# Entry of the feed-forward part of a hybrid layer: order of the first sums, the norm and the last output-projection block

## The chip, the cores and the metric

The kernel runs on one core of one Trainium2 chip. The metric is the device time of one execution in microseconds (us); a kernel's time is the median of several executions.

## The reference

The kernel computes one inference step of one encoder layer, in float32, for 1024 prompt frames and 32 sample frames (1056 token columns in all). Eight heads of latent attention and eight heads of a recurrent mixer (RWKV-7) read the same normalised projection; their outputs are concatenated into `mix` (1024 wide). What matters here is the tail:

```python
mix = concat([rmsnorm(attn, attn_out_g), rw])
h = x + mix @ w_out                       # 1024 x 1024
u = rmsnorm(h, norm_ffn_g)
return h + (silu(u @ w_gate) * (u @ w_up)) @ w_down    # D_FF = 2816
```

## The kernel before, in words

The program has three stages, each with its own hand-written instruction stream per engine and semaphores between them: `layer_inputs` (projection, latents, recurrent mixer and sample attention), `prompt_attention`, and `tail`. All of the change lies in `tail` (L2081 to L2549). Data is held transposed: 128 features on the partitions and the 1056 tokens on the free axis, so a 1024-wide tensor is eight blocks of 128 x 1056.

**Output projection.** It is made in eight blocks `u` (L2215 to L2226), each of three column groups `n` of 352 tokens, each a chain of eight matmuls over `k` (blocks 0 and 1 have their upper four done in the attention stage already, so only four). Block `u` uses PSUM banks 3b to 3b+2 with b = u % 2, and the weight buffer `wo[b]`: there are two, `g.wo`, filled with blocks 0 and 1 by the stage before. SP loads block u into `wo[u % 2]` when block u-2 is done (L2159 to L2161), behind the loads of x (`hT`, in three parts), of `g_ffn` and of the first two units of feed-forward weights (L2147 to L2158). VectorE adds each bank to x in `hT` (L2425, semaphore `h_ok`), and after each block squares it (L2427) and adds the square to `acc` (L2428).

**The norm.** Its gain is applied at once and its row factor late. `uT` = `hT` times `g_ffn`, eight blocks, four by ScalarE (L2341) and four by VectorE (L2431), is written over `mixT`, so it has to wait until TensorE has read `mixT`. The row factor takes its own way: TensorE sums `acc` over the partitions (`row_sums`, L2227), VectorE scales and adds epsilon (L2440, L2441), GpSimd (POOL) raises to the power -0.5 (L2373), ScalarE spreads the nine columns into diagonal matrices (L2351), TensorE multiplies ones by them (`row_factors`, L2233), and VectorE copies the result to `rb` (L2448). Everything that leaves the first feed-forward products is then multiplied by `rb` on VectorE.

**The feed-forward products** are made by a Strassen-Winograd scheme: the 2 x 2 blocks of weights (A11, A12, A21, A22) and tokens (B11u, B12u, B21u, B22u; the first index is the upper or lower half of the features, the second the half of the columns, cut at HT = 528) give seven products with three sums of weights, S1, S2, S4 (and S3 in the place of A21), made by POOL for each unit (L2379 to L2384), and three sums of tokens, T1u, T2u, T4u (and T3 in the place of B12u), made once by VectorE (L2433 to L2437). A unit is a pair of 128-wide output blocks of the gate or of the up weights; `it` = 2u + nh counts units and column halves (NW = 264). For each `it` TensorE makes, in this order, X = A11 B11 (`p1_ps`), Y = S2 T2 (`p6_ps`), Z = S3 B12 (`p7_ps`), W = S1 T1 (`p5_ps`), then X += A12 B21, Z += A22 T4, W += S4 B22. `product` (L2239) records every one of these matmuls under L2241; each product is four matmuls of 264 columns, which the trace shows as eight.

In the first `it` TensorE waits for all of `h_ok` and for the four lower blocks of uT (`u_lo`) before X, makes `row_sums` behind X, and makes `row_factors` ahead of the second `it`. POOL's program begins with the power (it waits for `ms_ok`), and its sums for unit 0 come behind it:

```python
        pool.wait_ge(s["ms_ok"], 2)                                                        # L2372
        tt(row_ms[:, :], row_ms[:, :], minus_half, ALU.pow).then_inc(s["r_ok"], 1)
        for u in range(UNITS):
            ...
            pool.wait_ge(s[f"w_in{b}"], 32 * (u // 2 + 1))
            tt(S1, A21, A22, ALU.add).then_inc(s["s1_ok"], 1)
```

The order on every engine is written out by hand, so each engine does its instructions strictly in the order of its program.

Of the kernel before, what the change touches and what calls it, by code (L numbers as in the profile page):

```python
# [7 lines left out]
ALU = mybir.AluOpType  # L8
ACT = mybir.ActivationFunctionType
# [2071 lines left out]
def tail(nc, g, io, phase):  # L2081
# [20 lines left out]
    g11 = sb("g11", [P, NW])  # L2102
    diag = hid_[:, 9 * TOK:9 * TOK + TT_ * P].rearrange("p (t n) -> p t n", t=TT_)
    ones = hid_[:, 6 * TOK:6 * TOK + P]
    wo = [w[:, :, :] for w in g.wo]

    u_sum = [sb(f"u_sum{i}", [P, KH * HT]) for i in range(3)]
    wA = [sb(f"wA{i}", [P, 2 * KD * P + 3 * KH * P]) for i in range(2)]
# [18 lines left out]
    S1d = u_sum[1][:, 3 * NW:3 * NW + 10 * P].rearrange("p (k n) -> p k n", k=10), u_sum[2][:, FH * P:12 * P].rearrange("p (k n) -> p k n", k=1)  # L2127
    Alo, Ahi = (w[:, 0:FB * P].rearrange("p (k n) -> p k n", k=FB) for w in wA)

    names = """x_in0 x_in1 x_in2 g_in in0 in1 waited zero ps_done h_ok sq_ok acc_ok ssq_ps ms_ok r_ok diag_ok rb_ps rb_ok u_lo u_hi h_st  # L2130
        t1_ok t2_ok t3_ok t4_ok w_in0 w_in1 s1_ok s2_ok s3_ok s4_ok p1_ps p6_ps p7_ps p5_ps x_ps z_ps w_ps
        p1_ok y_done u3_ok c22_ok x_done z_done w_done th11 th22 th21 th12 c_ok hid_ok
        a11_in a12_in a21_in a22_in e1_ok e2_ok e3_ok e4_ok f1_ok f2_ok f3_ok f4_ok q1_ps q6_ps q7_ps q5_ps q4_ps q2_ps q3_ps
# [9 lines left out]
    def _(sp):  # L2143
        def load(u, b):
            sp.dma_start(wo[b], io.w_out[u]).then_inc(s[f"in{b}"], 16)

        for i, (a, b) in enumerate(X_PARTS):  # L2147
            sp.dma_start(hT[:, a:b], io.x_cols[a:b].rearrange("k p n -> p k n")).then_inc(s[f"x_in{i}"], 16)
        sp.dma_start(g_ffn[:, :], io.g_ffn).then_inc(s["g_in"], 16)

        def load_unit(u):
# [4 lines left out]

        load_unit(0)
        load_unit(1)  # L2158
        for u in range(2, KD):  # L2159
            sp.wait_ge(s["ps_done"], 3 * (u - 1))  # L2160
            load(u, u % 2)  # L2161
        sp.wait_ge(s["h_ok"], 3 * KD)
        sp.dma_start(io.y.rearrange("k p n -> p k n"), hT).then_inc(s["h_st"], 16)
        for u in range(2, UNITS):
# [49 lines left out]
    def _(pe):  # L2214
        for u in range(KD):  # L2215
            b = u % 2
            if u >= 2:
                pe.wait_ge(s[f"in{b}"], 16 * (u // 2))
            for n in range(3):
                if u >= 2:  # L2220
                    pe.wait_ge(s["h_ok"], 3 * (u - 2) + n + 1)
                depth = KD if u >= 2 else 4
                for k in range(depth):
                    last = pe.matmul(pb[3 * b + n][:, 0:TN], wo[b][:, k, :], g.mixT[:, k, n * TN:(n + 1) * TN],  # L2224
                                     start=k == 0 and u >= 2, stop=k == depth - 1, skip_group_check=u < 2)
                last.then_inc(s["ps_done"], 1)  # L2226
        def row_sums():  # L2227
            pe.wait_ge(s["acc_ok"], KD)
            for t, w in enumerate(width):
# [16 lines left out]
        for u in range(UNITS):  # L2246
            b = u % 2
            pe.wait_ge(s[f"w_in{b}"], 32 * (u // 2 + 1))
            for nh in range(2):
                it, c = 2 * u + nh, slice(nh * NW, nh * NW + NW)  # L2250
                X, Y, Z, W = (4 * (it % 2) + i for i in range(4))
                half = lambda t: (lambda k: t[:, k, c])
                left = lambda w: (lambda k: w[:, k, :])
                A11, A12, S3, A22 = (ab[b][:, a, KH * d:KH * d + KH] for a in range(2) for d in range(2))
                if it == 0:
                    pe.wait_ge(s["h_ok"], 3 * KD)
                    pe.wait_ge(s["u_lo"], KH)
                if it == 1:
                    row_factors()
                    pe.wait_ge(s["rb_ok"], 3)  # L2260
                if it >= 2:
                    pe.wait_ge(s["x_done"], it - 1)
                product(X, left(A11), half(B11u), KH, "p1_ps")
                if it == 0:
                    row_sums()
                pe.wait_ge(s["s2_ok"], u + 1)
                if it == 0:
                    pe.wait_ge(s["t2_ok"], 1)
                if it >= 2:
                    pe.wait_ge(s["y_done"], it - 1)  # L2270
                product(Y, left(sw[b][:, 1]), half(T2u), KH, "p6_ps")
                pe.wait_ge(s["s3_ok"], u + 1)
                if it == 0:
                    pe.wait_ge(s["t3_ok"], 1)
                if it >= 2:
                    pe.wait_ge(s["z_done"], it - 1)
                product(Z, left(S3), half(B12u), KH, "p7_ps")
                pe.wait_ge(s["s1_ok"], u + 1)
                if it >= 2:
                    pe.wait_ge(s["w_done"], it - 1)  # L2280
                product(W, left(sw[b][:, 0]), half(T1u), KH, "p5_ps")
                pe.wait_ge(s["p1_ok"], it + 1)
                product(X, left(A12), half(B21u), KH, "x_ps", first=False)
                if it == 0:
                    pe.wait_ge(s["t4_ok"], 1)
                pe.wait_ge(s["u3_ok"], it + 1)
                product(Z, left(A22), half(T4u), KH, "z_ps", first=False)
                pe.wait_ge(s["s4_ok"], u + 1)
                pe.wait_ge(s["c22_ok"], it + 1)
                product(W, left(sw[b][:, 2]), half(B22u), KH, "w_ps", first=False)  # L2290
# [43 lines left out]

    @block.scalar
    def _(act):
        act.wait_ge(s["ps_done"], 3 * KD)
        act.wait_ge(s["g_in"], 16)
        for k in (0, 1, 4, 5):
            act.wait_ge(s["h_ok"], 3 * k + 3)  # L2340
            act.activation(uT[:, k, :], hT[:, k, :], ACT.Copy, scale=g_ffn[:, k:k + 1]).then_inc(s["u_hi" if k >= KH else "u_lo"], 1)  # L2341
        for u in range(UNITS):
            for nh in range(2):
                it = 2 * u + nh
# [24 lines left out]
    @block.gpsimd  # L2369
    def _(pool):  # L2370
        tt = pool.tensor_tensor
        pool.wait_ge(s["ms_ok"], 2)  # L2372
        tt(row_ms[:, :], row_ms[:, :], minus_half, ALU.pow).then_inc(s["r_ok"], 1)  # L2373
        for u in range(UNITS):
            b = u % 2
            A11, A12, A21, A22 = (ab[b][:, a, KH * d:KH * d + KH] for a in range(2) for d in range(2))
            S1, S2, S4 = (sw[b][:, i] for i in range(3))
# [29 lines left out]
    def _(dve):  # L2407
# [7 lines left out]
        dve.memset(ones, 1.0).then_inc(s["zero"], 1)  # L2415
        dve.memset(row_ms[:, :], 1.0).then_inc(s["zero"], 1)
        dve.wait_ge(s["zero"], 3)
        for u in range(KD):
            for i, (a, _) in enumerate(X_PARTS):
                if u == a:  # L2420
                    dve.wait_ge(s[f"x_in{i}"], 16)
            for n in range(3):
                c = slice(n * TN, (n + 1) * TN)
                dve.wait_ge(s["ps_done"], u * 3 + n + 1)
                tt(hT[:, u, c], pb[3 * (u % 2) + n][:, 0:TN], hT[:, u, c], ALU.add).then_inc(s["h_ok"], 1)  # L2425
            dve.wait_ge(s["h_ok"], u * 3 + 3)
            named(tt(hsq, hT[:, u, :], hT[:, u, :], ALU.mult), "sq_ok", u + 1)  # L2427
            named(tt(acc, acc, hsq, ALU.add), "acc_ok", u + 1)  # L2428
        dve.wait_ge(s["g_in"], 16)
        for k in (2, 3, 6, 7):  # L2430
            dve.tensor_scalar(uT[:, k, :], hT[:, k, :], g_ffn[:, k:k + 1], None, ALU.mult).then_inc(s["u_hi" if k >= KH else "u_lo"], 1)  # L2431
        dve.wait_ge(s["u_lo"], KH)
        named(tt(T1u, B12u, B11u, ALU.subtract), "t1_ok", 1)  # L2433
        dve.wait_ge(s["u_hi"], KH)
        named(tt(T2u, B22u, T1u, ALU.subtract), "t2_ok", 1)
        tt(B12u, B22u, B12u, ALU.subtract).then_inc(s["t3_ok"], 1)
        tt(T4u, B21u, T2u, ALU.subtract).then_inc(s["t4_ok"], 1)  # L2437
        full = TOK // P
        dve.wait_ge(s["ssq_ps"], 1)
        dve.tensor_scalar(row_ms[:, 0:full], pb[6][:, 0:full], 1.0 / D, EPS, ALU.mult, ALU.add).then_inc(s["ms_ok"], 1)  # L2440
# [234 lines left out]
```

## Time and profile before

| | |
|---|---|
| median of 3 runs | 1986.47 us (1984.15 to 1988.41) |
| the profiled execution's own time | 1982.82 us |
| its span in the profile | 1981.0 us |
| TensorE busy with matmuls | 1841.3 us (93%) |
| VectorE, ScalarE, POOL busy | 1000.0, 361.7, 688.0 us |
| mean granted TensorE clock | 0.967 of full |

Engines: PE is TensorE's matmuls, PEld its weight loads, DVE is VectorE, ACT is ScalarE, POOL is GpSimd, SP is SyncE, whose rows are issues of DMAs. Times in rows are microseconds from the start of the span, and a bracket at the end of a row says how long the engine had been idle and whose instruction ended that. The granted clock PEclk is a share of 2.4 GHz, so 0.5 is 1.2 GHz. The `tail` stage begins at about 1006.7 us.

### The profile page before, as it was taken

To read this page: it belongs to the slowest core of one execution; us is meant where nothing else is said; L and a number is where in the kernel's file an instruction comes from. 1 tells how busy PE (TensorE), PEld (TensorE's weight loads), DVE (VectorE), ACT (ScalarE), POOL (GpSimd) and SP (SyncE) were. 2 spreads that over 40 slices of the span, in tenths; PEclk is the share of its full clock that TensorE was granted. 3 is DMA by queue.
4 is the path that set the end of the run, shared out by engine and by line. 5 is a ranking of instruction groups with operands and counts; after the bars stand their busy time and mean duration, and the time that the engine had idled before them with its cause. 6 is when DMAs were issued, how large, how long until landed. Compare 5 with 4: busy or idle time off the path is not lost. (4 is left out here: it accounts for less than half of the span.)

```text
span 1981.0 us, 33700 instructions
## 1 busy us (share of the span) xinstructions
PE 1841.3 (93%) x14303; PEld 1362.0 (69%) x14303; DVE 1000.0 (50%) x1742; ACT 361.7 (18%) x898; POOL 688.0 (35%) x495
## 2 busy tenths in 40 slices
PE   6799899999999796999989799999999999899998
PEld 3456566556566664555556488888888888688887
DVE  0657677677676785555533434343443443423522
ACT  1322332332323332333300100000000000000000
POOL 2543544544543453644500212222222221352622
PEclk9999999999999798999989899999999999899999
DMA  9545455554542101610031201111111111233331
GB/s 387 170 154 181 144 160 160 166 160 148 177 150 76 52 8 32 163 43 11 1 151 43 88 22 43 43 43 43 43 43 43 43 43 51 91 125 110 125 102 63
DMA packets 74071, 193.26 MB, mean 98 GB/s; under 512 B 19641, under 2 KB 48137, under 8 KB 66882
## 3 DMA queue, kind: packets, MB, share of 16 engines
q1 hardware_dynamic: 66578, 114.23, 18.2%
q10 hardware_dynamic: 7344, 76.88, 11.2%
q8 instruction: 114, 1.87, 0.4%
q14 instruction: 35, 0.29, 0.1%
HBM read 162.97 MB, written 20.44 MB: 93 GB/s over the span
## 5 line engine op out<-in xcount | busy, mean ns | idle before, releaser
L2241 PE MATMUL psum<-mixT,wA 128*128 128x264 f32 x1408 | 337.9, 388 | 6.3 <-DVE mixT L2431 4.8
L393 PE MATMUL psum<-wsl,xt 128*128 128x368 f32 x868 | 308.3, 496 | 5.2 <-ACT proj L869 4.1
L2241 PE MATMUL psum<-u_sum,wA 128*128 128x264 f32 x1232 | 299.0, 388 | 9.6 <-POOL wA L2381 9.6
L2241 PEld LDWEIGHTS psum<-mixT,wA 128*128 128x128 f32 x1408 | 269.2, 191 | 53.4 <-issue 5.3
L2241 PEld LDWEIGHTS psum<-u_sum,wA 128*128 128x128 f32 x1232 | 235.1, 191 | 50.1 <-POOL wA L2381 9.7
L393 PEld LDWEIGHTS psum<-wsl,xt 128*128 128x128 f32 x868 | 159.7, 196 | 105.9 <-issue 23.9
L2379 POOL TENSOR_TENSOR wA<-wA 128x512 f32<-128x512 f32 x22 | 27.9, 1267 | 401.1 <-DMA wA<-in_w_gate 203.3
L2241 PE MATMUL psum<-hid,wA 128*128 128x264 f32 x528 | 121.5, 386 | 2.1 <-DVE hid L2499 1.5
L2241 PEld LDWEIGHTS psum<-hid,wA 128*128 128x128 f32 x528 | 100.2, 190 | 19.9 <-issue 2.8
L2224 PE MATMUL psum<-mixT,wo 128*128 128x352 f32 x336 | 104.2, 474 | 7.0 <-PEq L2562 4.6
L2224 PEld LDWEIGHTS psum<-mixT,wo 128*128 128x128 f32 x336 | 66.0, 197 | 44.9 <-issue 8.3
L2241 PE MATMUL psum<-mixT,u_sum 128*128 128x264 f32 x352 | 83.9, 396 | 9.2 <-POOL u_sum L2398 9.1
L2392 POOL TENSOR_TENSOR u_sum<-wA 128x1280 f32<-128x1280 f32 x8 | 24.8, 3103 | 185.2 <-DMA wA<-in_w_down 185.2
L2041 DVE TENSOR_REDUCE part<-psum 128x1 f32<-128x80 f32 (+6 forms) x112 | 49.7, 469 | 75.8 <-PE psum L1835 73.3
L2241 PEld LDWEIGHTS psum<-mixT,u_sum 128*128 128x128 f32 x352 | 68.5, 195 | 22.6 <-POOL u_sum L2398 10.5
L1185 POOL TENSOR_TENSOR Ls<-Lraw,con 128x512 f32<-128x512 f32 x45 | 50.6, 1133 | 77.7 <-ACT Lraw L869 77.7
L1835 PE MATMUL psum<-kT,qT 96*128 96x144 f32 (+6 forms) x224 | 67.6, 461 | 7.6 <-DMA kT<-scratch_kT 7.6
L1854 PE MATMUL psum<-qT,kT 128*128 128x512 f32 (+6 forms) x224 | 71.4, 474 | 0.0
L1151 POOL TENSOR_TENSOR st<-st,con 128x3 f32<-128x3 f32 (+1 forms) x18 | 47.8, 2654 | 66.1 <-DVE st L1430 33.9
L2347 ACT ACTIVATE p<-psum 128x264 f32<-128x264 f32 x44 | 17.1, 390 | 257.5 <-PE psum L2241 257.3
L2462 DVE TENSOR_TENSOR part<-psum,p 128x264 f32<-128x264 f32 x44 | 19.0, 432 | 87.3 <-PE psum L2241 87.3
L2003 POOL TENSOR_TENSOR tot<-tot,pT 128x832 f32<-128x832 f32 (+5 forms) x48 | 61.7, 1286 | 3.8
(360 smaller groups left out, 2854.6 us busy)
## 6 DMA issues: line engine op xcount, KB each, us to landing
wsl<-in_w_in ACTq DMA_DIRECT2D x51, 1472.0 KB, 7.9
wA<-in_w_down SPq DMA_DIRECT2D x32, 704.0 KB, 4.1
wA<-in_w_gate SPq DMA_DIRECT2D x22, 512.0 KB, 4.3
wA<-in_w_up SPq DMA_DIRECT2D x22, 512.0 KB, 4.4
mixed<-proj SPq DMA_DIRECT2D x8, 784.0 KB
xt<-in_x_tiles SPq DMA_DIRECT2D x9, 512.0 KB, 12.0
wsl<-in_w_in SPq DMA_DIRECT2D x3, 1472.0 KB, 11.4
out_y<-hid SPq DMA_DIRECT2D x1, 4224.0 KB, 12.0
```

Source lines behind the costliest of these rows:

```text
L393: return pe.matmul(out, lhsT, rhs, start=start, stop=stop)
L1151: tt(out, ms, c_("minus_half")[:, 0:n], ALU.pow).then_inc(s[ok], 1)
L1185: tt(Ls[i % 2][:, :, :], Lraw[:, :, :], bcast(c_("levels")[:, i * 64:(i + 1) * 64], 1, H), ALU.mult).then_inc(s["Ls_ok"], 1)
L1835: pe.matmul(bank(pos)[:, 0:y - x], qT[b][0:QKD, t * P:(t + 1) * P], kT[b][0:QKD, x:y], start=True, stop=True).then_inc(s["a_ps"], 1)
L1854: pe.matmul(bank(pos)[0:size[k], 0:y - x], kT[b][:, k * P:k * P + size[k]], qT[b][:, x:y], start=True, stop=True).then_inc(s["b_ps"], 1)
L2003: step(pool.tensor_tensor(out[:, first[k]:], out[:, first[k]:], p[:, at[k]:at[k + 1]], ALU.add))
L2041: last = dve.tensor_reduce(part[:, t, slot:slot + 1], src[:, 0:w], AX.X, ALU.max)
L2224: last = pe.matmul(pb[3 * b + n][:, 0:TN], wo[b][:, k, :], g.mixT[:, k, n * TN:(n + 1) * TN], start=k == 0 and u >= 2, stop=k == depth - 1 ...
L2241: ins = pe.matmul(pb[bank][:, 0:NW], left(k), right(k), start=first and k == 0, stop=k == depth - 1, skip_group_check=not first)
L2379: tt(S1, A21, A22, ALU.add).then_inc(s["s1_ok"], 1)
L2392: tt(S1d[0], Ahi[:, 0:10], Ahi[:, FH:FH + 10], ALU.add)
L2462: named(tt(u2, Y, p1_[it % 2][:, :], ALU.add), "y_done", it + 1)
```

## The change

Five things are changed in `tail`, and nothing is added to or taken from the arithmetic except that four elementwise multiplications are cut in two halves each.

1. Two more weight buffers `wo[2]` and `wo[3]` in an unused part of `hid`. SP loads blocks 2 and 3 into them between the parts of x, and blocks 4 to 7 when block u-4 is done.
2. Block 7 runs first over k = 0 to 3 for its three column groups, then over k = 4 to 7. A semaphore `lo_read` tells that the lower half of `mixT` has been read, and `uT` blocks 0 to 3, and T1u from them, are then made during the second half of block 7. The upper blocks of uT are made in two column halves, the right one first.
3. In the first `it` TensorE no longer waits for block 7's `h_ok` ahead of X; W = S1 T1 comes second instead of fourth, and `row_sums` comes behind the first four products.
4. VectorE makes the square of block 7 and its sum last, behind T4u.
5. POOL's power stands ahead of its third unit instead of ahead of its first.

```diff
-    wo = [w[:, :, :] for w in g.wo]
+    wo = [w[:, :, :] for w in g.wo] + [hid_[:, (7 + i) * TOK:(7 + i) * TOK + KD * P].rearrange("p (k n) -> p k n", k=KD) for i in range(2)]
@@ block.sync
         for i, (a, b) in enumerate(X_PARTS):
             sp.dma_start(hT[:, a:b], io.x_cols[a:b].rearrange("k p n -> p k n")).then_inc(s[f"x_in{i}"], 16)
+            if i:
+                load(i + 1, i + 1)
...
-        for u in range(2, KD):
-            sp.wait_ge(s["ps_done"], 3 * (u - 1))
-            load(u, u % 2)
+        for u in range(4, KD):
+            sp.wait_ge(s["ps_done"], 3 * (u - 3))
+            load(u, u % 4)
@@ block.tensor
-                pe.wait_ge(s[f"in{b}"], 16 * (u // 2))
...
+                pe.wait_ge(s[f"in{u % 4}"], 32 if u >= 6 else 16)
+            parts = [(0, 4)] if u < 2 else [(0, KD)] if u < KD - 1 else [(0, 4), (4, KD)]
+            for first, end in parts:
+                for n in range(3):
+                    if u >= 2 and first == 0:
+                        pe.wait_ge(s["h_ok"], 3 * (u - 2) + n + 1)
+                    for k in range(first, end):
...
+                    if end == parts[-1][1]:
+                        last.then_inc(s["ps_done"], 1)
+                if len(parts) > 1 and first == 0:
+                    last.then_inc(s["lo_read"], 1)
...
                 if it == 0:
-                    pe.wait_ge(s["h_ok"], 3 * KD)
+                    pe.wait_ge(s["h_ok"], 3 * (KD - 1))
                     pe.wait_ge(s["u_lo"], KH)
                 if it == 1:
+                    pe.wait_ge(s["h_ok"], 3 * KD)
                     row_factors()
...
                 product(X, left(A11), half(B11u), KH, "p1_ps")
                 if it == 0:
-                    row_sums()
+                    pe.wait_ge(s["s1_ok"], 1)
+                    pe.wait_ge(s["t1_ok"], 1)
+                    pe.wait_ge(s["h_ok"], 3 * (KD - 1) + 1)
+                    product(W, left(sw[b][:, 0]), half(T1u), KH, "p5_ps")
...
                 product(Z, left(S3), half(B12u), KH, "p7_ps")
-                pe.wait_ge(s["s1_ok"], u + 1)
-                if it >= 2:
-                    pe.wait_ge(s["w_done"], it - 1)
-                product(W, left(sw[b][:, 0]), half(T1u), KH, "p5_ps")
+                if it == 0:
+                    row_sums()
+                    pe.wait_ge(s["u_hi"], KH)
+                else:
+                    pe.wait_ge(s["s1_ok"], u + 1)
+                    if it >= 2:
+                        pe.wait_ge(s["w_done"], it - 1)
+                    product(W, left(sw[b][:, 0]), half(T1u), KH, "p5_ps")
@@ block.scalar
+        def weighted(k, c, ok):
+            act.wait_ge(s["h_ok"], 3 * k + 3)
+            act.activation(uT[:, k, c], hT[:, k, c], ACT.Copy, scale=g_ffn[:, k:k + 1]).then_inc(s[ok], 1)
+
+        act.wait_ge(s["g_in"], 16)
+        act.wait_ge(s["lo_read"], 1)
+        for k in (0, 1):
+            weighted(k, slice(0, TOK), "u_lo")
         act.wait_ge(s["ps_done"], 3 * KD)
-        act.wait_ge(s["g_in"], 16)
-        for k in (0, 1, 4, 5):
-            act.wait_ge(s["h_ok"], 3 * k + 3)
-            act.activation(uT[:, k, :], hT[:, k, :], ACT.Copy, scale=g_ffn[:, k:k + 1]).then_inc(s["u_hi" if k >= KH else "u_lo"], 1)
+        for k in (4, 5):
+            weighted(k, slice(HT, TOK), "u_hi1")
+        for k in (4, 5):
+            weighted(k, slice(0, HT), "u_hi")
@@ block.gpsimd
-        pool.wait_ge(s["ms_ok"], 2)
-        tt(row_ms[:, :], row_ms[:, :], minus_half, ALU.pow).then_inc(s["r_ok"], 1)
         for u in range(UNITS):
+            if u == 2:
+                pool.wait_ge(s["ms_ok"], 2)
+                tt(row_ms[:, :], row_ms[:, :], minus_half, ALU.pow).then_inc(s["r_ok"], 1)
@@ block.vector
+        for u in range(KD - 1):
+            residual(u)
+            squares(u)
         dve.wait_ge(s["g_in"], 16)
-        for k in (2, 3, 6, 7):
-            dve.tensor_scalar(uT[:, k, :], hT[:, k, :], g_ffn[:, k:k + 1], None, ALU.mult).then_inc(s["u_hi" if k >= KH else "u_lo"], 1)
+        dve.wait_ge(s["lo_read"], 1)
+        for k in (2, 3):
+            weighted(k, slice(0, TOK), "u_lo")
         dve.wait_ge(s["u_lo"], KH)
         named(tt(T1u, B12u, B11u, ALU.subtract), "t1_ok", 1)
-        dve.wait_ge(s["u_hi"], KH)
+        residual(KD - 1)
+        dve.wait_ge(s["h_ok"], 3 * KD)
+        for k in (6, 7):
+            weighted(k, slice(HT, TOK), "u_hi1")
+        dve.wait_ge(s["u_hi1"], KH)
         named(tt(T2u, B22u, T1u, ALU.subtract), "t2_ok", 1)
         tt(B12u, B22u, B12u, ALU.subtract).then_inc(s["t3_ok"], 1)
+        for k in (6, 7):
+            weighted(k, slice(0, HT), "u_hi")
+        dve.wait_ge(s["u_hi"], KH)
         tt(T4u, B21u, T2u, ALU.subtract).then_inc(s["t4_ok"], 1)
+        squares(KD - 1)
```

Here `residual(u)` is the loop over n around L2425, and `squares(u)` the three lines from L2426 to L2428.

## Rows read from the trace of the kernel before

**Rows 1.** The page's 40 slices of the span: TensorE busy, granted clock (tenths).

```profile
PE   6799899999999796999989799999999999899998
...
PEclk9999999999999798999989899999999999899999
```

**Rows 2.** Waits between 1000 and 1160 us: in total, times, longest.

```profile
POOL row_ms L2373 <- DVE row_ms L2441: 129.8, 1, 129.8
...
PE psum L2241 <- POOL wA L2381: 9.6, 1, 9.6
...
PE psum L2241 <- DVE mixT L2431: 4.8, 1, 4.8
...
PE psum L2224 <- DMA wo<-in_w_out: 2.4, 1, 2.4
```

**Rows 3.** Timeline around output-projection block 2: start, duration, engine, line, instruction, idle before.

```profile
1024.00 0.52 DVE L2425 TENSOR_TENSOR hid<-psum,hid 128x352 f32<-128x352 f32 x1 [1.84 <-PE psum L2224]
...
1026.37 68.93 PE L2224 MATMUL psum<-mixT,wo 128*128 128x352 f32 x227 [2.41 <-DMA wo<-in_w_out]
...
1032.98 0.52 DVE L2425 TENSOR_TENSOR hid<-psum,hid 128x352 f32<-128x352 f32 x1 [5.87 <-PE psum L2224]
```

**Rows 4.** DMA issues between 1006 and 1017 us: size, issue to landing.

```profile
hid<-in_x_cols SPq DMA_DIRECT2D x1, 2112.0 KB, 12.2
hid<-in_x_cols SPq DMA_DIRECT2D x1, 1584.0 KB, 7.4
```

**Rows 5.** Windows: length, busy of PE, PEld, DVE, ACT, POOL, granted clock, DMA.

```profile
1026.00:1029.40 3.40, 3.03 (x5) 1.85 (x6) 1.11 (x1) 0.00 (x0) 0.00 (x0) 0.50 0.24 92
...
1125.00:1133.28 8.28, 0.00 (x0) 0.00 (x1) 3.78 (x4) 2.59 (x9) 4.34 (x4) 0.50 0.05 20
```

**Rows 6.** Timeline of the feed-forward entry, 1099 to 1152 us, all engines.

```profile
1099.18 0.52 DVE L2425 TENSOR_TENSOR hid<-psum,hid 128x352 f32<-128x352 f32 x1 [4.21 <-PE psum L2224]
...
1113.38 0.52 DVE L2425 TENSOR_TENSOR hid<-psum,hid 128x352 f32<-128x352 f32 x1 [4.21 <-PE psum L2224]
1113.38 4.37 ACT L2341 ACTIVATE mixT<-hid,g_ffn 128x1056 f32<-128x1056 f32 x4 [111.81 <-PE psum L2224]
...
1113.94 1.26 DVE L2427 TENSOR_TENSOR hid<-hid 128x1056 f32<-128x1056 f32 x1
...
1116.52 2.81 DVE L2431 TENSOR_SCALAR mixT<-hid,g_ffn 128x1056 f32<-128x1056 f32 x4
...
1118.12 3.70 PE L2241 MATMUL psum<-mixT,wA 128*128 128x264 f32 x8 [4.78 <-DVE mixT L2431]
...
1121.66 2.00 PE L2230 MATMUL psum<-hid 128*128 128x1 f32 x18
...
1126.30 2.35 DVE L2437 TENSOR_TENSOR u_sum<-mixT,u_sum 128x2112 f32<-128x2112 f32 x1
...
1128.86 1.80 POOL L2373 TENSOR_TENSOR row_ms<-row_ms,con 128x9 f32<-128x9 f32 x1 [129.78 <-DVE row_ms L2441]
...
1130.69 2.74 ACT L2351 ACTIVATE hid<-con,row_ms 128x128 f32<-128x128 f32 x9 [8.44 <-POOL row_ms L2373]
...
1133.28 3.89 PE L2241 MATMUL psum<-u_sum,wA 128*128 128x264 f32 x8 [9.62 <-POOL wA L2381]
...
1139.59 1.94 PE L2241 MATMUL psum<-u_sum,wA 128*128 128x264 f32 x8
...
1141.37 1.94 PE L2241 MATMUL psum<-mixT,wA 128*128 128x264 f32 x8
...
1146.71 2.28 PE L2236 MATMUL psum<-hid 128*128 128x128 f32 x18
...
1150.54 2.05 PE L2241 MATMUL psum<-mixT,wA 128*128 128x264 f32 x8 [1.55 <-DVE rb L2448]
```

**Rows 7.** VectorE busy in one window of the output projection.

```profile
1038.00:1100.00 62.00, 17.30 (x23) 1.00 0.10 34
```

**Rows 8.** Timeline: a VectorE and a POOL instruction side by side in unit 1.

```profile
1170.64 1.27 POOL L2382 TENSOR_TENSOR wA<-wA 128x512 f32<-128x512 f32 x1
1170.96 1.24 DVE L2491 SCALAR_TENSOR_TENSOR hid<-hid,part 128x264 f32<-128x264 f32 x1
```

More of the change, by code:

```diff
@@ L2128, in tail @@
     Alo, Ahi = (w[:, 0:FB * P].rearrange("p (k n) -> p k n", k=FB) for w in wA)
-    names = """x_in0 x_in1 x_in2 g_in in0 in1 waited zero ps_done h_ok sq_ok acc_ok ssq_ps ms_ok r_ok diag_ok rb_ps rb_ok u_lo u_hi h_st
+    names = """x_in0 x_in1 x_in2 g_in in0 in1 in2 in3 lo_read u_hi1 waited zero ps_done h_ok sq_ok acc_ok ssq_ps ms_ok r_ok diag_ok rb_ps rb_ok u_lo u_hi h_st
         t1_ok t2_ok t3_ok t4_ok w_in0 w_in1 s1_ok s2_ok s3_ok s4_ok p1_ps p6_ps p7_ps p5_ps x_ps z_ps w_ps
@@ L2217, in _ @@
             if u >= 2:
-                pe.wait_ge(s[f"in{b}"], 16 * (u // 2))
[L2219 to L2226, printed above, removed]
+                pe.wait_ge(s[f"in{u % 4}"], 32 if u >= 6 else 16)
[5 more added lines that the diff above has]
+                    for k in range(first, end):
+                        last = pe.matmul(pb[3 * b + n][:, 0:TN], wo[u % 4][:, k, :], g.mixT[:, k, n * TN:(n + 1) * TN],
+                                         start=k == 0 and u >= 2, stop=k == end - 1, skip_group_check=u < 2 or len(parts) > 1)
+                    if end == parts[-1][1]:
+                        last.then_inc(s["ps_done"], 1)
+                if len(parts) > 1 and first == 0:
+                    last.then_inc(s["lo_read"], 1)
         def row_sums():
@@ L2417, in _, with residual @@
         dve.wait_ge(s["zero"], 3)
-        for u in range(KD):
+        def residual(u):
             for i, (a, _) in enumerate(X_PARTS):
@@ L2425, in _, with squares @@
                 tt(hT[:, u, c], pb[3 * (u % 2) + n][:, 0:TN], hT[:, u, c], ALU.add).then_inc(s["h_ok"], 1)
+        def squares(u):
             dve.wait_ge(s["h_ok"], u * 3 + 3)
@@ L2428, in _, with weighted @@
             named(tt(acc, acc, hsq, ALU.add), "acc_ok", u + 1)
+        def weighted(k, c, ok):
+            dve.tensor_scalar(uT[:, k, c], hT[:, k, c], g_ffn[:, k:k + 1], None, ALU.mult).then_inc(s[ok], 1)
+        for u in range(KD - 1):
+            residual(u)
+            squares(u)
         dve.wait_ge(s["g_in"], 16)
-        for k in (2, 3, 6, 7):
-            dve.tensor_scalar(uT[:, k, :], hT[:, k, :], g_ffn[:, k:k + 1], None, ALU.mult).then_inc(s["u_hi" if k >= KH else "u_lo"], 1)
+        dve.wait_ge(s["lo_read"], 1)
+        for k in (2, 3):
+            weighted(k, slice(0, TOK), "u_lo")
         dve.wait_ge(s["u_lo"], KH)
         named(tt(T1u, B12u, B11u, ALU.subtract), "t1_ok", 1)
-        dve.wait_ge(s["u_hi"], KH)
+        residual(KD - 1)
[3 more added lines that the diff above has]
+        dve.wait_ge(s["u_hi1"], KH)
         named(tt(T2u, B22u, T1u, ALU.subtract), "t2_ok", 1)
         tt(B12u, B22u, B12u, ALU.subtract).then_inc(s["t3_ok"], 1)
+        for k in (6, 7):
+            weighted(k, slice(0, HT), "u_hi")
+        dve.wait_ge(s["u_hi"], KH)
         tt(T4u, B21u, T2u, ALU.subtract).then_inc(s["t4_ok"], 1)
+        squares(KD - 1)
         full = TOK // P
```

## The prediction

> **What bounds the kernel now.** I read the 40 slices first. TensorE is busy nine tenths and more of nearly every slice from the tail's start at 1006.7 us (slice 21 of 49.5 us each) to the end, with dents in slices 21 and 23, and the granted clock dips in the same slices [rows 1]. So the tail is bound by TensorE, and only holes in its stream, or stretches at the lower clock, can be won. Second, the waits of the tail's first 160 us: TensorE stands idle 2.4 us for a DMA of output weights, 4.8 us for the weighted h (`uT`) and 9.6 us for POOL's sums of weights [rows 2]. Third, the timeline says why. Block 7's last bank is read at 1113.38; then come VectorE's squares, its uT, X at 1118.12, the row sums at 1121.66 and a hole until 1133.28 [rows 6]. The hole is named after POOL, but POOL had stood idle for 129.8 us in front of the power [rows 2]: it waited for `ms_ok`, which VectorE writes only behind T4u, at 1128.6. The sums of weights, which need only loaded weights, were queued behind it. Fourth, the clock: after the holes it is 0.50, that is 1.2 GHz instead of 2.4 [rows 5], and the product at 1118.12 lasts 3.70 and that at 1133.28 3.89 us, against 1.94 later [rows 6].
>
> **Part 1, the two weight buffers.** Before, TensorE finishes block 1 at about 1024.0, waits 2.41 us and restarts at the lower clock: block 2's first bank is read at 1032.98 [rows 3]. At the pace of later banks (14.20 us for three, 1099.18 to 1113.38 [rows 6], so 4.73 each) it would be read at 1024.00 + 4.73 = 1028.73. The stall costs 4.25 us in all: 2.4 of waiting, 1.85 of slow matmuls. After, block 2's load stands behind 1584 KB of x, which landed 7.4 us after its issue (about 1014.6), ahead of 2112 KB which took until about 1019.8 [rows 4]. That pace, 2112 KB in 5.2 us, gives 512 KB in 1.3 us: block 2 lands at about 1016, 8 us early. Block 3 lands before 1024 and is wanted at 1038; the feed-forward weights come 2.6 us later and are wanted at 1113; block 4 is issued when bank 3 is done, at 1016.9, and wanted at 1052. SP issues two more DMAs ahead of the third part of x, some 0.4 us each, which that slack covers. Gain: 4.25 us, of which 1.85 is the clock. Bounds: 2.4 (the clock falls all the same) and 4.3.
>
> **Part 2, POOL's sums first.** Eight instructions of 1.27 us move from 1130 to 1140 into the time after the weights land, some 1026 to 1037. They can slow VectorE: beside one of them a 264-column instruction lasts 1.24 us [rows 8] where its kind takes 0.43. VectorE is busy only 17.3 of 62 us there [rows 7], and TensorE wants a bank back 14 us after it was filled, so the cost is nothing; without that cover it would be under 10 us. S1, S2, S3 then never make TensorE wait. What is late next is the sums of tokens, and then the norm.
>
> **Part 3, the new order, followed through** (in the clock of the old trace, 4.25 us aside).
> - Block 7 starts at 1113.35 - 14.20 = 1099.15; its lower half ends at 1106.25. ScalarE's two weighted blocks at 4.37 / 4 = 1.09 each end at 1108.5, VectorE's two (0.70 each) earlier; T1u takes 2.35: 1110.9. Then the first two residual adds, and the third at 1113.38 as before, done 1113.93.
> - TensorE goes from block 7 into X at 1113.35 without a hole (1.78 us a product at full clock, 1139.59 to 1141.37 [rows 6]) and into W: 1116.9.
> - Right halves of uT: VectorE two of 0.35, ScalarE two of about 0.6 (estimates: half of the full ones plus a little), done 1114.7. T2u until 1117.1, T3 until 1119.4, two left halves 0.7, T4u 2.35 until 1122.5, and the two squares' instructions 1116.52 - 1113.94 = 2.6: 1125.1.
> - TensorE: Y from 1117.15, Z from 1119.45 to 1121.25 (waits of 0.2 and 0.5 us), then **a new hole of 3.85 us** until acc is ready at 1125.1. Row sums 2.0: 1127.1.
> - Norm chain: scaling 0.3, then power to last diagonal as before, 1130.69 + 2.74 - 1128.86 = 4.57: 1132.0.
> - TensorE meanwhile: X, Z, W, 3 x 1.78 = 5.34, plus what the clock costs. Before, three products from 1133.28 took until 1141.37, that is 8.09 instead of 5.34: 2.75 us lost; after the 2.41 us stall 1.85 was lost. Here the 2.0 us of row sums stand first in the slow stretch, so I take 1.9. End 1134.35, behind the norm chain, which is therefore covered.
> - `row_factors` to the first product of the second `it`: 1150.54 - 1146.71 = 3.83. So that product starts at 1138.2, where it was 1150.54.
>
> Gain: 12.3 us. As a check: holes were 4.8 + 9.6, are 4.55 (9.85 less); slow clock cost about 1.8 + 2.75, costs 1.9 (2.65 less); 12.5. Bounds on the clock's price: nothing (end 1132.4, gain 14.3) and all three products at 1.2 GHz (5.34 us, gain 8.9).
>
> A hole of 3.85 us is longer than the 2.41 us after which the clock read 0.50 [rows 3, 5]; that is why I charge for it. The Trainium skill says the same in "TensorE: Matmul & The Clock Gate", section "HAM oscillation": an array left waiting falls back and each resumed burst starts slow again. By that rule the gain is 12.3; if waits beside row sums were harmless it would be 14.3.
>
> **What costs nothing.** The first half of block 7 costs no more than before: the same 48 recorded matmuls, each with its own weight load. The store of h to HBM is issued at 1113.93 as before, since its wait is for the same add. From the second `it` on nothing is changed, and TensorE is the bound to the end, so the whole gain stays.
>
> **Sum.** 4.25 + 12.3 = 16.6 us. The profiled execution took 1982.82 us (span 1981.0), so its like would take 1966.2; it lay 3.65 us under the median of the three runs, and the median would be 1986.47 - 16.6 = 1969.9 us.
>
> **The rivals.**
> - *A, the clock is not paid* (10%): it holds through the hole, or is back before the three products. For it: after the 1.55 us wait at 1150.54 the product takes 2.05 us, so full clock. Against: 2.41 us was enough once. Gain 18.5, 1968.0 us.
> - *B, a longer slow stretch* (13%): the small waits at 1116.9 and 1119.0 plus the hole plus row sums, whose matmuls have one column, leave the clock at 1.2 GHz until `row_factors`. For it: the products from 1133.28 on lost 2.75 us, more than I charge here. Gain 8.9 + 4.25 = 13.1, 1973.3 us; with the wait for `rb` as another fall, 1.9 more, 1975.2 us. The Trainium skill, same page, section "A second HAM failure mode: psum-queue depth-cycling", has short waits between groups of matmuls doing this.
> - *C, one of the two halves does nothing* (3%): block 2's load still arrives late, or something I hold for covered ends the wait at the entry. Landing at 1016 against a need at 1024 speaks against the first. A gain of 4 us or less, 1982.2 us or above.
> - *D, slower* (2%): the clock, once down at the hole, stays at 1.2 GHz beyond the entry. A low clock loses half of its length, so it decides after 2 x 16.6 = 33 us beyond what is charged: low until about 1165, the change loses. Each `it` of seven products takes 7 x 1.78 = 12.5 us at full clock, so with one more `it` low it would be 1986.5 + 12.5 = 1999 us. Against it: the dearest restart shown lost 2.75 us, 5.5 us at half speed.
>
> **How the numbers follow.** The forecast has 72%, A 10, B 13, C 3, D 2. The likeliest case gives 1969.9 us. The range takes in A with the scatter of the runs (2 to 2.5 us each way) and B: 1965.0 to 1976.0. A measurement of this kernel can tell some 0.2%, 4 us. All but D and C gain more: faster 0.95, same 0.03, slower 0.02.
>
> **What would show it.** In the profile after: no wait for a DMA at block 2 and full clock through it; POOL's eight sums near 1026 to 1037, and the power idle-waiting until about 1123 (4.25 earlier than 1127.4); no hole between block 7 and X; a hole of about 3.9 us ahead of the row sums, ended by VectorE's L2428 counterpart; products slow behind it for about 4 us; `row_factors` without a wait for ScalarE. It would be wrong if the row sums wait much longer than 4 us (VectorE's halves cost more than I estimated), if TensorE waits for the diagonals (then the norm chain is the bound), or if the time from the second `it` to the end is not that of before.

## The result, and the profile after

The first set of runs gave 1970.89 us in the median of 8 (1963.90 to 1978.12) against 1983.74 us for the kernel before in the same set (8 runs, 1981.13 to 1988.41). The ratio is 0.9933 with a 95% interval of 0.9907 to 0.9959, which is 8 to 18 us. Two later sets gave 0.9925 (0.9903 to 0.9946) and 0.9924 (0.9902 to 0.9947). The profiled execution took 1963.90 us, its span 1962.1, against 1982.82 and 1981.0 before. Three executions in the later sets (2037.58, 2717.59 and 2026.48 us) ran at a lower granted clock than all others (0.92, 0.65 and 0.92) and count in no ratio.

The spans differ by 18.9 us, more than the medians (12.9). Part of that is no effect of the change: the tail begins at 1003.38 us here and at 1006.73 before, with identical code ahead of it. All stage times below are therefore taken inside the tail. "Add" is the start of the last residual add of block 7, "second pass" the first product of the second `it`. The spans are printed to 0.1 us, so the last two columns hold to that here and below; the two columns before them hold to 0.01.

| profile | tail starts | start to add | add to second pass | second pass to end | tail in all |
|---|---|---|---|---|---|
| before | 1006.73 | 106.65 | 37.16 | 830.46 | 974.27 |
| after | 1003.38 | 102.68 | 26.50 | 829.54 | 958.72 |
| less | | 3.97 | 10.66 | 0.92 | 15.55 |

The page's slices of busy TensorE and granted clock, the counterpart of [rows 1]: the dents at slices 21 and 23 are gone from both rows. What is left of the holes is too short to show in slices of 49 us; it shows in the waits and windows below.

```profile
PE   6899899899999797899999999999999999899998
...
PEclk9899999999999798999999999999999999999999
```

The waits between 1000 and 1160 us of the kernel after (total, times, longest), the counterpart of [rows 2]:

```profile
POOL row_ms L2398 <- DVE row_ms L2483: 88.1, 1, 88.1
...
PE psum L2237 <- DVE hid L2454: 3.6, 1, 3.6
...
PE psum L2248 <- DVE rb L2490: 1.5, 1, 1.5
...
PE psum L2248 <- DVE u_sum L2473: 0.5, 1, 0.5
PE psum L2248 <- DVE mixT L2474: 0.4, 1, 0.4
```

The waits of 2.4, 4.8 and 9.6 us are gone. POOL still waits 88 us for `ms_ok`, but nobody waits for what stands behind it. A new wait of 3.6 us stands at the row sums (L2237), ended by the last sum into `acc` (L2454).

The timeline around block 2, the counterpart of [rows 3]:

```profile
1020.65 28.56 PE L2227 MATMUL psum<-mixT,hid 128*128 128x352 f32 x96
1020.86 0.53 DVE L2449 TENSOR_TENSOR hid<-psum,hid 128x352 f32<-128x352 f32 x1 [1.84 <-PE psum L2227]
...
1021.71 2.09 POOL L2403 TENSOR_TENSOR wA<-wA 128x512 f32<-128x512 f32 x1 [25.97 <-DMA wA<-in_w_gate]
1022.71 2.21 DVE L2454 TENSOR_TENSOR hid<-hid 128x1056 f32<-128x1056 f32 x1
...
1025.66 0.53 DVE L2449 TENSOR_TENSOR hid<-psum,hid 128x352 f32<-128x352 f32 x1 [0.74 <-PE psum L2227]
```

The window of block 2 (length, busy time of PE, PEld, DVE, ACT, POOL, granted clock, DMA share, GB/s), and the size and time to landing of its load, which was issued at 1004.22:

```profile
1020.65:1034.90 14.25, 14.25 (x50) 9.16 (x49) 5.04 (x5) 0.00 (x0) 11.64 (x8) 1.00 0.38 151
...
hid<-in_w_out SPq DMA_DIRECT2D x1, 512.0 KB, 8.2
```

The load landed at about 1012.4, 8.2 us before block 2 begins. Block 2 follows without a wait and at full clock, and its first bank is read 4.80 us after block 1's last one, where it was 8.98 before. POOL's sums now lie here. Where they meet VectorE's sum into `acc`, both sides take longer (2.09 for 1.27, 2.21 for 1.26 us), and nobody waits for either.

The timeline of the entry after the change, the counterpart of [rows 6]:

```profile
1099.00 2.24 ACT L2354 ACTIVATE mixT<-hid,g_ffn 128x1056 f32<-128x1056 f32 x2 [100.78 <-PE psum L2227]
...
1101.28 2.36 DVE L2467 TENSOR_TENSOR u_sum<-mixT 128x2112 f32<-128x2112 f32 x1 [0.77 <-ACT mixT L2354]
...
1105.85 1.94 PE L2248 MATMUL psum<-mixT,wA 128*128 128x264 f32 x8
1106.06 0.53 DVE L2449 TENSOR_TENSOR hid<-psum,hid 128x352 f32<-128x352 f32 x1 [1.43 <-PE psum L2227]
1106.06 2.62 ACT L2354 ACTIVATE mixT<-hid,g_ffn 128x528 f32<-128x528 f32 x4 [4.81 <-PE psum L2227]
...
1107.55 2.36 DVE L2473 TENSOR_TENSOR u_sum<-mixT,u_sum 128x2112 f32<-128x2112 f32 x1
...
1110.06 2.02 PE L2248 MATMUL psum<-u_sum,wA 128*128 128x264 f32 x8 [0.48 <-DVE u_sum L2473]
...
1112.45 2.02 PE L2248 MATMUL psum<-mixT,wA 128*128 128x264 f32 x8 [0.37 <-DVE mixT L2474]
1113.15 2.36 DVE L2478 TENSOR_TENSOR u_sum<-mixT,u_sum 128x2112 f32<-128x2112 f32 x1
...
1116.71 1.26 DVE L2454 TENSOR_TENSOR hid<-hid 128x1056 f32<-128x1056 f32 x1
...
1118.02 3.22 PE L2237 MATMUL psum<-hid 128*128 128x1 f32 x18 [3.56 <-DVE hid L2454]
...
1121.17 3.88 PE L2248 MATMUL psum<-mixT,wA 128*128 128x264 f32 x8
...
1121.65 1.79 POOL L2398 TENSOR_TENSOR row_ms<-row_ms,con 128x9 f32<-128x9 f32 x1 [88.14 <-DVE row_ms L2483]
...
1124.85 2.26 PE L2248 MATMUL psum<-u_sum,wA 128*128 128x264 f32 x8
...
1128.73 2.28 PE L2243 MATMUL psum<-hid 128*128 128x128 f32 x18
...
1132.56 2.05 PE L2248 MATMUL psum<-mixT,wA 128*128 128x264 f32 x8 [1.55 <-DVE rb L2490]
```

X runs straight behind block 7 and Y waits 0.48 us for T2u. Then the hole: TensorE has done four products by 1114.46 and waits until VectorE, behind T4u, has made the two instructions of the squares. The row sums and the product at 1121.17 are slow, and part of the product at 1124.85. The windows of the hole, of the row sums and of the three products behind (length, busy time of PE, PEld, DVE, ACT, POOL, granted clock, DMA share, GB/s):

```profile
1114.46:1118.02 3.56, 0.01 (x1) 0.00 (x0) 3.48 (x3) 0.00 (x0) 0.00 (x0) 1.00 1.02 411
1118.02:1121.20 3.18, 3.18 (x19) 3.15 (x19) 0.00 (x0) 0.00 (x0) 0.00 (x0) 0.60 0.03 9
1121.17:1128.70 7.53, 7.53 (x26) 6.14 (x25) 1.44 (x5) 2.73 (x9) 1.79 (x1) 0.71 0.00 0
```

The granted clock reads 1.00 through the hole itself. It is lower only behind it, once the matmuls have started again.

### The profile page after: what moved, and what is told of

It reads as the page before. It is cut to its first block and busy times, and to the rows that moved or that the text cites. A ratio compares the mean times of both kernels' runs of the same rounds, so it can differ in the third digit from the quotient of the medians.

```text
span 1962.1 us, 33708 instructions
## 1 busy us (share of the span) xinstructions
PE 1834.7 (94%) x14303; PEld 1357.4 (69%) x14303; DVE 1002.4 (51%) x1744; ACT 362.1 (18%) x900; POOL 690.4 (35%) x495
## 5 line engine op out<-in xcount | busy, mean ns | idle before, releaser
L2248 PEld LDWEIGHTS psum<-mixT,u_sum 128*128 128x128 f32 x352 | 67.8, 193 | 22.3 <-POOL u_sum L2422 10.6
L1835 PEld LDWEIGHTS psum<-kT,qT 96*128 96x128 f32 x224 | 42.5, 197 | 30.1 <-DMA kT<-scratch_kT 7.9
L869 ACT ACTIVATE proj<-psum,rstd 128x368 f32<-128x368 f32 x54 | 30.5, 565 | 174.9 <-PE psum L393 174.9
L1854 PEld LDWEIGHTS psum<-qT,kT 128*128 128x128 f32 x224 | 39.7, 183 | 31.5 <-issue 20.1
```

What stands on the lines that cost most here:

```text
L869: copy = lambda out, in_, **k: act.activation(out, in_, ACT.Copy, **k)
L1835: pe.matmul(bank(pos)[:, 0:y - x], qT[b][0:QKD, t * P:(t + 1) * P], kT[b][0:QKD, x:y], start=True, stop=True).then_inc(s["a_ps"], 1)
L1854: pe.matmul(bank(pos)[0:size[k], 0:y - x], kT[b][:, k * P:k * P + size[k]], qT[b][:, x:y], start=True, stop=True).then_inc(s["b_ps"], 1)
L2248: ins = pe.matmul(pb[bank][:, 0:NW], left(k), right(k), start=first and k == 0, stop=k == depth - 1, skip_group_check=not first)
```

## The experiments

Eleven runs of eight kernels were made, in three sets, each beside the kernel before. Medians of different sets are not compared; the times inside the tail are.

### The changed kernel again

No edit.

> The changed kernel once more, unaltered. Its eight runs fell into two groups, 1963.9 to 1966.2 us and 1975.5 to 1978.1 us, with nothing between; the kernel before had none this far apart (1981.1 to 1988.4). Theory S (two courses of the same program): the runs fall into the same two groups again, about 11 us apart, and a profile of a run of the upper group shows one place with some 11 us more, or the clock at half speed for some 22 us more, than in the profile of the lower group. Rival R (chance): the runs fill the space between 1964 and 1978 us.

Measured: median 1968.58 us, ratio 0.9925 (0.9903 to 0.9946). The runs that count lay at 1967.1, 1967.5, 1968.5, 1968.6, 1972.4 and 1975.2, all inside the gap between the two groups (1966.2 to 1975.5), so theory S falls and rival R stands. The profile's tail was 958.7 us, as in the first, while it started at 1008.10 instead of 1003.38. A third profile of the same kernel (the repeat below) has a start of 1014.59 and again a tail of 958.7. These three profiles show one course of the tail: its length was the same within 0.1 us, and in them the scatter comes from ahead of it, from code that the change does not touch. What makes the earlier stages scatter was not looked for.

### One part at a time

The two buffers on the kernel before (item 1 of the change with its loads and waits, and nothing else):

> The kernel before with the two weight buffers alone. My theory: block 2 follows block 1 without a wait and at full clock, 4.0 to 4.3 us less than before, nothing else moves. Rival (the clock falls all the same): 2.4 us. Rival (the stall is only moved): 0. If the two groups of run times show here as well, 11 us apart, the buffers are what brings them.

POOL's order on the kernel before (item 5 of the change and nothing else):

> The kernel before with POOL's power alone moved behind the sums of its first two units. My theory: product Y starts when T2u is ready (10.7 us after the last residual add instead of 19.9), so about 9 us of hole go; the norm chain ends at the same time as before and is covered by the products; gain 9.5 to 11 us, most of the whole change's gain at the entry. Rival (the norm chain ends the wait now): row_factors waits for ScalarE's diagonals, and the gain is limited to the time from the diagonals' end (1133.4) to row_factors' start (1146.7), 13 us at most, less what the products need. If the two groups show here, this edit brings them.

The changed kernel without the buffers (item 1 taken back):

> The changed kernel without the two weight buffers: blocks 2 to 7 are loaded into two buffers as before. My theory: the 2.4 us wait and the slow matmuls behind it are back, 4.0 to 4.3 us slower than the changed kernel; the entry takes 26.5 us from the last residual add to the second pass, as in the changed kernel. Rival: the two groups of times vanish, which would put them down to the buffers or to the stretches in the weights' loads.

Both parts on the kernel before, and a repeat of it:

> The kernel before with the two weight buffers and POOL's power moved, and nothing else: block 7 whole, old order of the products, squares of block 7 first. In the profiles so far the time from the last residual add to the second pass is 37.2 us before, 26.5 in the changed kernel and 26.0 with POOL's power alone moved. Theory P (POOL's order is the whole gain at the entry, the split and the new order of products and squares give nothing net): the tail lasts as long as the changed kernel's, 958.7 us in two profiles, within 1 us, and the median is the changed kernel's within the scatter. Rival N (the split gives some of it): 3 us or more slower than the changed kernel.

> Buffers and POOL's order alone, again. So far the entry took 25.95 us, and the first product behind the wait for rb ran at 1.2 GHz (3.58 us instead of 2.05), which made the rest 832.7 us instead of 829.5. Theory L (that fall of the clock is a matter of how the run lies): here the product takes 2.05 us, the rest 829.5, and the tail 958.2 us, half a microsecond under the changed kernel's. Rival O (the old order brings it, since TensorE has more to do at full clock before and less after): 3.4 to 3.6 us and a tail of 961 again. Median within 3 us of the changed kernel's either way.

The stage times of these profiles, worked out as in the table above, and the ratios, each from its own set:

| kernel | start to add | add to second pass | second pass to end | tail | ratio to before |
|---|---|---|---|---|---|
| before | 106.65 | 37.16 | 830.46 | 974.27 | 1 |
| buffers alone | 102.64 | 35.94 | 832.42 | 971.00 | 0.9983 (0.9963 to 1.0002) |
| POOL's order alone | 106.58 | 25.96 | 829.70 | 962.24 | 0.9949 (0.9932 to 0.9965) |
| changed, without buffers | 106.91 | 26.38 | 830.92 | 964.21 | 0.9948 (0.9933 to 0.9963) |
| both alone | 102.72 | 25.95 | 832.67 | 961.34 | 0.9916 (0.9888 to 0.9944) |
| both alone, repeat | 102.70 | 25.95 | 832.42 | 961.07 | 0.9922 (0.9896 to 0.9947) |
| changed | 102.68 | 26.50 | 829.54 | 958.72 | 0.9933 (0.9907 to 0.9959) |

The buffers take 3.9 to 4.2 us out of the first stage, in each of the three pairs with and without them; where they are taken out of the changed kernel, a wait of 2.3 us for the DMA is back. In the whole tail they are worth 3.3 us alone, only about 1 us on top of POOL's order, and 5.5 on top of the other edits, because matmuls further on are slow in some of these kernels and not in others: the product behind the wait for `rb`, and the one behind the 7.7 us hole of the down projection, both below. By medians the kernel with the buffers alone can't be told from the one before. POOL's order alone takes 11.2 us out of the entry, a little over what was expected of it (9.5 to 11), where the whole change takes 10.7; `row_factors` did not wait for the diagonals, so the rival fell. The timeline of TensorE with POOL's order alone:

```profile
1121.58 3.86 PE L2241 MATMUL psum<-mixT,wA 128*128 128x264 f32 x8 [4.78 <-DVE mixT L2432]
1125.23 2.21 PE L2230 MATMUL psum<-hid 128*128 128x1 f32 x18
1127.60 2.02 PE L2241 MATMUL psum<-u_sum,wA 128*128 128x264 f32 x8 [0.15 <-DVE u_sum L2436]
...
1129.99 2.02 PE L2241 MATMUL psum<-mixT,wA 128*128 128x264 f32 x8 [0.37 <-DVE mixT L2437]
...
1138.97 2.28 PE L2236 MATMUL psum<-hid 128*128 128x128 f32 x18
```

Its last add is at 1116.84. The old hole of 4.78 us ahead of X and the slow X are there; what is gone is everything from the row sums on. In the changed kernel the early hole is closed, and one of 3.56 us with slow matmuls behind it is opened at the row sums. The split of block 7, the halves of `uT` and the new orders of TensorE and VectorE together thus cost 0.55 us at the entry (26.50 against 25.95), and without the buffers 0.42 (26.38 against 25.96).

Theory P said "within 1 us" for the tail; the two profiles of both parts alone were 2.6 and 2.4 us over, so it holds for the entry, within that 0.55 us, and not for the tail: the difference lies behind the entry. Theory L is refuted too: the product behind the wait for `rb` was slow again. From the timelines of the repeat of the two parts alone:

```profile
1139.28 3.60 PE L2243 MATMUL psum<-mixT,wA 128*128 128x264 f32 x8 [1.55 <-DVE rb L2451]
1142.68 2.12 PE L2243 MATMUL psum<-u_sum,wA 128*128 128x264 f32 x8
...
1697.06 7.98 PE L2243 MATMUL psum<-mixT,u_sum 128*128 128x264 f32 x22 [7.71 <-POOL u_sum L2401]
```

and the counterpart of its last row in the changed kernel:

```profile
1688.66 6.84 PE L2248 MATMUL psum<-mixT,u_sum 128*128 128x264 f32 x22 [7.71 <-POOL u_sum L2422]
```

The product at 1139.28 is followed 3.40 us later instead of 1.88, the next 1.95 instead of 1.78, and the one behind the 7.7 us hole of the down projection lasts 1.14 us longer: 2.8 of the 2.9 us of that stage. That is rival O as far as it says that the fall comes again. The old order by itself does not bring it: the kernel before, and the one with POOL's order alone, have that order and ran this product at full clock (2.05 us), and the one with the buffers alone ran it slow (3.40). Why it comes with the old order and the buffers together was not shown: the 1.55 us of waiting are the same in all of them.

### The price of the hole

```diff
                 if it == 0:
+                    for _ in range(2):
+                        for k in range(KH):
+                            pe.matmul(pb[7][:, 0:NW], A11[:, k, :], B11u[:, k, c], start=k == 0, stop=k == KH - 1)
                     row_sums()
```

> The changed kernel with sixteen more recorded matmuls (two products A11 B11 into an unused bank, results thrown away) in the hole ahead of the row sums. Theory C (the hole costs through the clock as well): TensorE is busy 3.56 us in a hole of 3.56 us, the clock stays at full; row sums take 2.0 instead of 3.2 us and the three products behind 5.3 instead of 7.6, so the second pass starts 3.4 us earlier after the last residual add (23.1 us instead of 26.5). Rival (the wait is harmless): 26.5 us stays. Rival (the row sums themselves let the clock fall): the products behind are slow all the same, some 25 us.

Measured: 23.26 us from the add to the second pass, 3.24 less than the changed kernel; the tail is 955.1 us against 958.7, so the kernel with useless work in it is the faster one; ratio to before 0.9906 (0.9877 to 0.9935). The timeline of TensorE:

```profile
1123.49 3.72 PE L2292 MATMUL psum<-mixT,wA 128*128 128x264 f32 x16
...
1127.21 2.10 PE L2237 MATMUL psum<-hid 128*128 128x1 f32 x18
...
1129.24 2.05 PE L2248 MATMUL psum<-mixT,wA 128*128 128x264 f32 x8
```

The windows of the row sums and of the three products behind:

```profile
1127.21:1129.24 2.03, 2.03 (x20) 2.00 (x19) 0.00 (x0) 0.00 (x0) 0.00 (x0) 1.00 0.03 13
1129.24:1134.68 5.44, 5.44 (x26) 4.66 (x25) 1.44 (x5) 2.74 (x9) 1.79 (x1) 1.00 0.00 0
```

With useless work in the hole the row sums start at the same distance from the add (1127.21 - 1115.25 = 11.96 us, as 1118.02 - 1106.06) and everything behind is at full clock. The 3.56 us hole therefore cost a further 3.24 us through the clock. Theory C holds, and both rivals fall. The Trainium skill's rule ("TensorE: Matmul & The Clock Gate", section "HAM oscillation") agrees: an array left waiting starts its next burst slow, and here one that is kept busy does not.

### Where the squares stand

VectorE's squares of block 7 moved between T3 and T4u:

```diff
         tt(B12u, B22u, B12u, ALU.subtract).then_inc(s["t3_ok"], 1)
+        squares(KD - 1)
...
         tt(T4u, B21u, T2u, ALU.subtract).then_inc(s["t4_ok"], 1)
-        squares(KD - 1)
```

> The changed kernel with VectorE's squares of block 7 between T3 and T4u instead of last. Theory Q (squares made last are what the row sums wait for, and T4u had slack): row sums start at 9.0 us after the last residual add instead of 12.0, the hole is 0.7 us, the clock stays, the norm chain ends at 17.2 us and is then what row_factors waits for; second pass at 21 us instead of 26.5, median 5.5 us under the changed kernel's. Rival (T4u is then late and its product waits): T4u is ready at 12.1 us, product Z at 12.7, so no; if its adds are slower than I hold, 1 to 2 us less gain.

The square on ScalarE, and only the sum on VectorE:

```diff
+        act.wait_ge(s["h_ok"], 3 * KD)
+        act.wait_ge(s["acc_ok"], KD - 1)
+        act.activation(hsq, hT[:, KD - 1, :], ACT.Square).then_inc(s["sq_ok"], 1)
...
         tt(B12u, B22u, B12u, ALU.subtract).then_inc(s["t3_ok"], 1)
+        dve.wait_ge(s["sq_ok"], KD)
+        named(tt(acc, acc, hsq, ALU.add), "acc_ok", KD)
...
         tt(T4u, B21u, T2u, ALU.subtract).then_inc(s["t4_ok"], 1)
-        squares(KD - 1)
```

> The changed kernel with the square of block 7 made by ScalarE behind its weighted halves (1.1 us, done at 3.7 us after the last residual add), and VectorE's sum into acc (1.3 us) between T3 and T4u. Theory Q: the row sums start without a hole at 8.2 us, TensorE is the bound, the norm chain ends at 15.7 just as the products do; second pass at 19.6 us instead of 26.5, median about 7 us under the changed kernel's and 20 under before. Rival (the norm chain ends later, because ScalarE's square delays its copy of X and VectorE's adds): 21 to 22 us.

Measured:

| kernel | add to second pass | second pass to end | tail | median | ratio to before |
|---|---|---|---|---|---|
| squares ahead of T4u | 20.85 | 830.66 | 954.07 | 1965.80 | 0.9895 (0.9872 to 0.9918) |
| square on ScalarE | 19.56 | 829.46 | 951.62 | 1960.35 | 0.9867 (0.9839 to 0.9894) |

Both in one set with a median of 1987.72 for the kernel before. From the timeline of the kernel with the square on ScalarE, whose last add is at 1114.08:

```profile
1116.60 1.07 ACT L2367 ACTIVATE hid<-hid 128x1056 f32<-128x1056 f32 x1
...
1120.24 1.25 DVE L2479 TENSOR_TENSOR hid<-hid 128x1056 f32<-128x1056 f32 x1
...
1122.33 1.99 PE L2237 MATMUL psum<-hid 128*128 128x1 f32 x18
...
1129.74 2.36 PE L2243 MATMUL psum<-hid 128*128 128x128 f32 x18
...
1133.64 2.05 PE L2248 MATMUL psum<-mixT,wA 128*128 128x264 f32 x8 [1.55 <-DVE rb L2494]
```

and from that with the squares only moved:

```profile
1122.45 2.10 PE L2237 MATMUL psum<-hid 128*128 128x1 f32 x18 [0.35 <-DVE hid L2454]
...
1134.54 2.05 PE L2248 MATMUL psum<-mixT,wA 128*128 128x264 f32 x8 [1.55 <-DVE rb L2490]
```

The row sums stand right behind the fourth product, 8.2 to 8.8 us after the add, and nothing behind them is slow. So theory Q holds in both kernels (21 and 19.6 us were expected, 20.85 and 19.56 measured), and the rivals fell. T4u had slack, as expected: its product waited for nothing with the square on ScalarE, and 0.28 us, ended by a VectorE sum behind T4u, with the squares moved.

To see this beside the changed kernel in one set, both were repeated:

> The changed kernel again, to stand beside the next two in one set of runs. The median under before's by 13 to 18 us; in the profile 26.5 us from the last residual add to the second pass and 829.5 from there to the end, 958.7 in all from the tail's start, as in the two profiles so far.

> The changed kernel with block 7's square on ScalarE and its sum ahead of T4u, again beside the other two. Entry 19.6 us, tail 951.7 us, 7 us under the changed kernel's; median 5 to 9 us under it and 18 to 26 under before's. If the clock falls at the wait for rb here too, 2 to 3 us of that are lost.

Measured, with 1986.01 us for the kernel before: the changed kernel 1970.76 (ratio 0.9924, 0.9902 to 0.9947), the two parts alone 1969.79 (0.9922, 0.9896 to 0.9947), the square on ScalarE 1961.78 (0.9877, 0.9853 to 0.9901). The tails are 958.7, 961.1 and 951.8 us. The version with the square on ScalarE beats the kernel before and the changed one: its slowest run (1964.37) lies under the changed kernel's fastest (1968.96), 9.0 us by medians and 7.0 by the tails, which is the surer figure. The changed kernel and the two parts alone can't be told apart by their medians.

## Why the prediction was right, and where it was off

The forecast was 1969.9 us, inside 1965 to 1976; measured was 1970.89. Such closeness is luck, for two errors cancel and the runs scatter by more than 10 us. The forecast started from 1986.47, the median of three runs, where eight runs gave 1983.74, and its gain of 16.6 us is 3.7 more than the 12.9 between the medians (interval 8 to 18). What can be checked more closely is the tail: the working gave 4.25 + 12.3 = 16.6 us less, the profiles give 15.55.

- **Part 1** held. Block 2's load is 8.2 us early (8 forecast), the clock reads 1.00 through the block, and the stage is 3.97 us shorter (4.25 forecast); the bound of 2.4, by which the clock falls all the same, was not met, and the load is not late.
- **Part 2** held. POOL's sums lie at 1021.7 to 1033.5 and no one waits for them; that they can slow VectorE and be slowed by it is shown, at no cost. One reading was off, to the safe side: a bank is wanted back not 14 us after it was filled but 23.7 (28.40 - 4.73), since two sets of three banks take turns. `row_factors` did not wait for the norm chain: its last diagonal ended at 1126.2, 2.5 us ahead of the start at 1128.73.
- **Part 3**, step by step from the last add. The forecast's steps are given from 1113.38 on: T2u ready at 3.7 (measured 3.85), T3 at 6.0 (6.24), acc at 11.7 (11.9), hole 3.85 (3.56), row sums' end 13.7 (15.1), three products' end 21.0 (22.7), second pass 24.8 (26.5). So the working was right within 0.3 us up to the start of the row sums, and of the 1.7 us missing at the end 1.4 came behind it.
- **The term that was mis-sized** is the clock's price at the new hole: "the 2.0 us of row sums stand first in the slow stretch, so I take 1.9". The runs showed that the row sums are slowed too: 3.15 us, against 2.0 at full clock, and the three products took 7.56 instead of 5.34. Together that is 3.4 us; taken away by the filler it was 3.24. The 2.0 us came from a row of before [rows 6] in which X, ahead of the row sums, had taken most of the slow stretch.
- **"The whole gain stays"** was nearly so: the rest of the tail is 0.92 us shorter. The product group behind the 7.7 us hole of the down projection took 6.84 us where it was 7.86:

```profile
1706.63 7.86 PE L2241 MATMUL psum<-mixT,u_sum 128*128 128x264 f32 x22 [7.71 <-POOL u_sum L2398]
```

- **The rivals.** A (the clock is not paid) and D (it stays low) fell by the windows. B (a longer slow stretch) overshot: the third product was at full clock. It pointed the right way, since 3.4 us were paid, between the 1.9 charged and its 5.3. C fell in both of its halves; its price, a gain of 4 us or less, fits only the half at the entry; a late load alone would have left the entry's 12.3.

One thing was not asked, and should have been: what each part was worth by itself. Part 2's gain was credited to "the new order, followed through" as a whole, 12.3 us, though the trace of before could price POOL's move alone. T2u is ready 10.6 us after the add there, and the old order of squares first has no hole at the row sums:

```profile
1121.63 2.36 DVE L2435 TENSOR_TENSOR u_sum<-mixT,u_sum 128x2112 f32<-128x2112 f32 x1
```

The runs say that this single edit takes 11.2 us out of the entry and the whole change 10.7, and that the remaining edits at the entry traded a hole of 4.78 us ahead of X for one of 3.56 us at the row sums, each with slow matmuls behind it. At the entry they pay only once the squares no longer stand last: then it takes 20.9 us, or 19.6 with the square on ScalarE, 6.4 less than with POOL's order alone. That the changed kernel's tail is nonetheless 2.4 to 2.6 us shorter than that of the two parts alone comes from matmuls behind the entry that are slow in the one and not in the other, and was not forecast.

## What to carry to other kernels

When an engine's program begins with an instruction that waits for the end of a long chain, look at what stands behind it and needs none of that chain; moving two instructions can be most of the gain. When work is pulled forward on one engine, follow what it pushes back on the same engine, and ask who waits for that: here two VectorE instructions of 1.26 us moved to the end, or one of them to an idle engine, decided about 7 us. Price a hole in TensorE's stream at its length and add something for slow matmuls behind it, small ones included. What to add is not a fixed share: here it was 1.85 us behind 2.41, 3.24 behind 3.56, 2.75 behind 9.62, and nothing or 1.7 behind 1.55. Price each part of a change alone before adding them up.

## What the runs showed of the hardware that was not expected

- In three profiles of the changed kernel the tail lasted 958.7 us, within 0.1, although it began at 1003.4, 1008.1 and 1014.6 us. The stretches at 1.2 GHz fell on nearly the same instructions each time. In the profiles, what the clock costs in a stage went with the kernel and not with the moment at which it ran.
- A wait of 1.55 us for `rb`, the same in all thirteen profiles, was followed by a slow product (3.40 to 3.60 us) in the three that have the old order and the buffers, and by one at full clock (2.05 us) in the ten others. The granted clock was full during the wait, and in `row_factors` ahead of it, in all thirteen. What tells the cases apart stayed open.
- A wait of 7.71 us in the down projection, also the same in all thirteen, was followed by a group of 22 recorded matmuls that lasted 6.67 to 6.94 us in seven profiles and 7.86 to 8.20 in six. Profiles of one kernel always fell on the same side. So 1 to 1.4 us of a difference between two tails can lie there, far from the edit; this too stayed open.
- Eighteen recorded matmuls of a single column take 2.0 us at full clock and 3.15 to 3.7 us behind a hole, and their weight loads are busy 2.00 us (the kernel with the filled hole) and 3.15 (the changed one). So weight loads with hardly any columns behind them are slowed by the clock as well.
